# Expert layer in two sweeps: coefficients kept in two tensors by token half, 14 up tiles run for half the tokens first, and every second late down tile turned by VectorE

## Chip, cores and metric

One core of one Trainium2 chip runs the whole program. The metric is device microseconds (us) from the first to the last instruction of one execution, as a median of several. TensorE (PE) multiplies and can also transpose; VectorE (DVE), ScalarE (ACT) and GpSimd (POOL) do elementwise work; SyncE (SP) issues most loads; 16 DMA engines move the data.

## What is computed

Two transformer blocks on 256 tokens of width 1024. The change touches only the last part, a layer of 16,384 experts, of which each token uses 8 heads x 16:

```python
def peer_ffn(h, w_query, sub_keys1, sub_keys2, expert_down, expert_up):
    ...
    gates = jax.nn.softmax(top_v, axis=-1).astype(h.dtype)
    ...
        u = jnp.take(expert_down, idx_blk, axis=0)
        act = jax.nn.gelu(jnp.einsum('bpd,bphkd->bphk', h_blk, u))
        vv = jnp.take(expert_up, idx_blk, axis=0)
        return jnp.einsum('bphk,bphkd->bpd', g_blk * act, vv)
```

## The kernel before

The kernel does not gather experts. It computes all of them as 128 tiles of 128 experts and multiplies the unused ones by a coefficient of zero.

**Down sweep.** For each tile `n` the rows of `expert_down` (512 KB) are loaded, turned so that the model dimension lies on partitions, split into a high part (ACT, `dT_high`) and a low part (DVE, `dT_low`), and multiplied with the split tokens: 8 blocks x 3 products = 24 matmuls of 128x256 (`pe_three`, L577, L579, L581). ACT applies gelu and stores `G[:, n, :]`, 128 experts x 256 tokens (L2550). An ordinary tile is turned by PE, 8 transposes into two PSUM banks (L1189), done two tiles ahead: PE's order is turn(n+2), down(n). Tiles in `SQUARED` (n above 49 with n % 5 equal to 1 or 3, 31 tiles) are loaded in four pieces of 128 KB arranged so that DVE's 32x32 transposes finish the turn (L2011, L2012); PE has no turn for them. `dT_raw` of a squared tile lies where `dT_low` of the same third lay, so its turn waits for the matmuls of tile n-3. DVE's order is set by `v_tile`: the low part of tile n, then the turn of tile n+2 if that is squared.

**Coefficients.** While the sweep runs, POOL adds the gates into a DRAM matrix `C_dram` (expert x token, 16 MB, zeroed before) with 256 indirect DMAs: 8 heads x 2 token halves x 16 picks. A half of a head waits until the 16 adds of the head before it, for the same tokens, have landed.

**Up sweep.** For each tile `p` SP loads 128 rows of `expert_up` (512 KB) and the tile's coefficients (128 KB), each into one of 4 buffers. The up load of tile p waits for `tile_done` of tile p-4 (PE has finished it); the coefficient load of tile p+1 follows right behind it on SP. DVE multiplies `G` by the coefficients (`v_gate`, L2057), ACT copies the high parts (`up_high` L2558, `A_high` L2564), DVE subtracts for the low parts (L1318), and PE does 12 matmuls of 128x512 into four PSUM banks that add up over all tiles: banks 0 and 1 for tokens 0 to 127, banks 2 and 3 for the others. DVE's order is gate(p+1), low part of up tile p, low part of A for p. All engines run lists written out by hand, in order, with semaphores between them; no scheduler moves anything.

Of the kernel before, what the change touches and what calls it, by code (L numbers as in the profile page):

```python
# [15 lines left out]
P = 128  # L16
# [102 lines left out]
def program(nc, ctx, I, out):  # L119
# [368 lines left out]
    C_dram = nc.dram_tensor("c_dram", [N_KEYS * N_KEYS * S, 1], F32, kind="Internal").ap()  # L488
    turn_banks = ((4, 5), (0, 1), (2, 3))
    SQUARED = [n for n in range(N_KEYS) if n > 49 and n % 5 in (1, 3)]  # L490
# [713 lines left out]
    def pe_up_part(p, b):  # L1204
        t, at = b // 2, slice(b % 2 * CW, (b % 2 + 1) * CW)
        return pe_three(bank[b], A_low[p][:, t * P:(t + 1) * P], A_high[p % 4][:, t * P:(t + 1) * P],
                        up_low[p % 4][:, at], up_hi[p % 4][:, at], p == 0, p == N_KEYS - 1)

    def pe_tile_up(p):
        pe.wait_ge(weighed, p + 1)  # L1210
        pe.wait_ge(up_split, p + 1)
        for b in range(4):
            m = pe_up_part(p, b)
        m.then_inc(tile_done, 1)

    def pe_last_tiles():
        pe.wait_ge(weighed, N_KEYS)
        pe.wait_ge(up_split, N_KEYS)
        for b in range(4):
            pe_up_part(N_KEYS - 2, b)  # L1220
            pe_up_part(N_KEYS - 1, b).then_inc(bank_summed, 1)

    def pe_experts():
        pe_tile_turn(0)
        pe_tile_turn(1)
        for n in range(N_KEYS):
            if n + 2 < N_KEYS and n + 2 not in squared_at:
                pe_tile_turn(n + 2)
            pe_tile_down(n)
        for b in range(4):  # L1230
            fill(("acc", b), b)
        for p in range(N_KEYS - 2):
            pe_tile_up(p)
        pe_last_tiles()
# [726 lines left out]
    def v_picks(c, part, ts=range(TT), hs=range(PAIRS)):  # L1961
# [20 lines left out]
        else:  # L1982
            v_own.settle(v.scalar_tensor_tensor(rank[:, 0, rows], sel_key[:, 0, rows], float(N_KEYS), sel_key[:, 1, rows],
                                                ALU.mult, ALU.add))
            for t in ts:
                own = slice(PAIRS * t + hs.start, PAIRS * t + hs.stop)
                v.tensor_scalar(places[:, TP * c + own.start:TP * c + own.stop, :], rank[:, 0, own, :], float(S),
                                tokens[:, t:t + 1], ALU.mult, ALU.add).then_inc(picks_ready, 1)
# [30 lines left out]
    def v_tile(n):  # L2019
# [4 lines left out]
        if n + 2 in squared_at:  # L2024
            v_square_turn(n + 2)
# [28 lines left out]
    def v_gate(p):  # L2054
# [4 lines left out]
    def v_split_up(p):  # L2059
        v.wait_ge(up_high, p + 1)  # L2060
        v_low(up_low[p % 4], up_tile[p % 4], up_hi[p % 4]).then_inc(up_split, 1)

    def v_weigh(p):
        v.wait_ge(gated, p + 1)
        v.wait_ge(a_high_made, p + 1)
        v_low(A_low[p], G[:, p, :], A_high[p % 4]).then_inc(weighed, 1)

    def v_experts():
# [4 lines left out]
        for p in range(N_KEYS):  # L2073
            if p + 2 < N_KEYS:
                v_gate(p + 2)
            if p + 1 < N_KEYS:
                v_split_up(p + 1)
                v_weigh(p + 1)
# [473 lines left out]
    def a_split_up(p):  # L2552
        a.wait_ge(up_in[p % 4], 16 * (p // 4 + 1))
        if p > 3:
            a.wait_ge(tile_done, p - 3)
        else:
            held(a, ("down", N_KEYS - 3 + p // 2))
        a.copy(up_hi[p % 4].bitcast(F32R), up_tile[p % 4]).then_inc(up_high, 1)  # L2558

    def a_weigh(p):  # L2560
        a.wait_ge(gated, p + 1)
        if p > 3:
            a.wait_ge(tile_done, p - 3)
        a.copy(A_high[p % 4].bitcast(F32R), G[:, p, :]).then_inc(a_high_made, 1)  # L2564

    def a_experts():
# [16 lines left out]
        for p in range(1, N_KEYS):  # L2583
            a_weigh(p)
            a_split_up(p)
# [53 lines left out]

    def g_experts():  # L2640
        g.wait_ge(zeroed, 16)
        for c in range(4):
            for h in range(PAIRS * c, PAIRS * (c + 1)):
                for t in range(TT):
                    if c == 0:
                        g.wait_ge(picks_ready, 2 * (TT * h + t + 1))
                    elif h % PAIRS == 0:
                        g.wait_ge(picks_ready, 8 + 3 * c)
                    if h:
                        g.wait_ge(scattered[t][(h - 1) % 2], 16 * TOPK * ((h - 1) // 2 + 1))  # L2650
# [54 lines left out]
    def s_chunks():  # L2705
        for i, (name, w, c0, n) in enumerate(chunks):
# [125 lines left out]
```

## Time and profile before

| | |
|---|---|
| median of 3 runs | 1539.0 us (1538.61 to 1540.46) |
| profiled execution | 1540.89 us, span 1539.6 us |
| PE busy | 1500.0 us, 97% of the span |
| DVE, ACT, POOL busy | 1081.1, 657.8, 434.8 us |
| mean granted TensorE clock | 0.992 of full speed |

The span is the time between the first and the last instruction in the trace; the execution's own time is 1.3 us more. A busy share is an average over very different stages. The down sweep ends and the up sweep begins at about 1183 us of the span.

### The profile page before, as it was taken

What the parts mean: (1) busy time and instruction counts of PE and PEld (TensorE: products, weight loads), DVE (VectorE), ACT (ScalarE), POOL (GpSimd) and SP (SyncE); (2) the same over time, 40 slices, a digit from 0 to 9 for tenths busy, and PEclk for the clock granted to TensorE, in tenths of its full rate; (3) what the DMA queues carried; (4) which work ended last, traced back from release to release, by engine and by line L of the source; (5) the groups of instructions that cost most, each with busy time, mean ns of one, the idle gap of its engine ahead of it and who ended that gap; (6) DMA issues with size and microseconds to landing.
All of it is one profiled execution on the core that took longest, in us unless ns stands there. A gap on an engine that the chain in (4) does not pass through costs nothing.

```text
span 1539.6 us, 25208 instructions
## 1 busy us (share of the span) xinstructions
PE 1500.0 (97%) x9851; PEld 1264.4 (82%) x9851; DVE 1081.1 (70%) x1895; ACT 657.8 (43%) x982; POOL 434.8 (28%) x285
## 2 busy tenths in 40 slices
PE   8999999999999888999999999999999999999998
PEld 5777878875755577599999999999999888888887
DVE  5788788664765754667988875656556777777776
ACT  4456453643321511343444443334334445455453
POOL 0000000000010200028888888888884000000000
PEclk9999999999999989999999999999999999999999
DMA  9777574357555920356767666666664777777776
GB/s 343 270 244 247 193 259 138 137 191 250 193 197 177 397 88 22 137 165 186 144 138 147 142 139 158 144 164 144 159 152 109 239 240 240 238 240 240 239 241 232
DMA packets 179850, 297.24 MB, mean 193 GB/s; under 512 B 51434, under 2 KB 88066, under 8 KB 179732
## 3 DMA queue, kind: packets, MB, share of 16 engines
q1 hardware_dynamic: 133072, 277.08, 53.8%
q0 software_dynamic: 39296, 8.55, 8.0%
q10 hardware_dynamic: 7364, 9.99, 2.0%
q8 instruction: 79, 1.29, 0.3%
q14 instruction: 39, 0.32, 0.1%
HBM read 276.54 MB, written 19.03 MB: 192 GB/s over the span
## 4 chain that ended last, share of the span: by engine, by line
PE 87%; DVE 5%; ACT 3%; issue 2%; DMA 2%; ACTq 1%; DVEq 0%
PE bank L577 22%; PE bank L579 22%; PE bank L581 21%; PE bank L1189 6%; PE bank L572 5%; PE bank L1120 1%; ACTq L2101 1%; PE bank L1136 1%; PE bank L549 1%; PE bank L927 1%; DVE gt L1299 1%; PE bank L939 1%; PE bank L938 1%; DVE w_low L1318 1%; PE bank L629 1%
## 5 line engine op out<-in xcount | busy, mean ns | idle before, releaser
L2653 POOL DMA_INDIRECT c_dram<-gates,places x256 | 412.4, 1611 | 149.6 <-issue 77.7
L577 PE MATMUL bank<-hT_high,dT_high 128*128 128x256 f32 x1024 | 296.0, 289 | 0.0
L579 PE MATMUL bank<-hT_low,dT_high 128*128 128x256 f32 x1024 | 289.0, 282 | 0.0
L581 PE MATMUL bank<-hT_high,dT_low 128*128 128x256 f32 x1024 | 285.6, 279 | 0.0
L2558 ACT CAST up_high<-slot 128x1024 fp32r<-128x1024 f32 x128 | 134.3, 1049 | 157.8 <-DMA slot<-in_expert_up_dram 157.8
L577 PE MATMUL bank<-up_high,A_high 128*128 128x512 f32 x512 | 200.0, 391 | 1.0 <-DVE A_low L1318 1.0
L579 PE MATMUL bank<-up_low,A_high 128*128 128x512 f32 x512 | 200.7, 392 | 0.0
L581 PE MATMUL bank<-up_high,A_low 128*128 128x512 f32 x512 | 199.2, 389 | 0.0
L577 PEld LDWEIGHTS bank<-hT_high,dT_high 128*128 128x128 f32 x1024 | 192.8, 188 | 4.6 <-issue 0.2
L581 PEld LDWEIGHTS bank<-hT_high,dT_low 128*128 128x128 f32 x1024 | 193.5, 189 | 0.0
L579 PEld LDWEIGHTS bank<-hT_low,dT_high 128*128 128x128 f32 x1024 | 192.6, 188 | 0.0
L1318 DVE TENSOR_TENSOR up_low<-slot,up_high 128x1024 fp32r<-128x1024 f32 x128 | 156.8, 1225 | 32.9 <-ACT up_high L2558 32.5
L2190 ACT CAST w_hi<-slot 128x2048 fp32r<-128x2048 f32 x51 | 97.0, 1902 | 137.7 <-PE bank L581 95.4
L1318 DVE TENSOR_TENSOR w_low<-slot,w_hi 128x2048 fp32r<-128x2048 f32 x51 | 116.7, 2288 | 45.6 <-ACT w_hi L2190 45.4
L1318 DVE TENSOR_TENSOR dT_low<-bank,dT_high 128x512 fp32r<-128x512 f32 x194 | 123.3, 677 | 25.7 <-ACT dT_high L2546 24.5
L577 PE MATMUL bank<-w_hi,h_hi 128*128 128x512 f32 x344 | 138.2, 402 | 0.0
L579 PE MATMUL bank<-w_low,h_hi 128*128 128x512 f32 x344 | 136.4, 396 | 0.0
L581 PE MATMUL bank<-w_hi,h_lo 128*128 128x512 f32 x344 | 135.3, 393 | 0.0
L2550 ACT ACTIVATE G<-bank 128x256 f32<-128x256 f32 x128 | 49.1, 384 | 194.0 <-PE bank L581 194.0
L577 PEld LDWEIGHTS bank<-up_high,A_high 128*128 128x128 f32 x512 | 96.2, 188 | 23.1 <-DVE A_low L1318 1.4
L581 PEld LDWEIGHTS bank<-up_high,A_low 128*128 128x128 f32 x512 | 96.1, 188 | 21.2
L579 PEld LDWEIGHTS bank<-up_low,A_high 128*128 128x128 f32 x512 | 96.1, 188 | 20.5
(454 smaller groups left out, 2545.9 us busy)
## 6 DMA issues: line engine op xcount, KB each, us to landing
slot<-in_expert_up_dram SPq DMA_DIRECT2D x128, 512.0 KB, 3.5
slot<-in_expert_down_dram SPq DMA_DIRECT2D x97, 512.0 KB, 3.7
slot<-in_w_in_dram SPq DMA_DIRECT2D x41, 1024.0 KB, 5.2
P<-in_w_ada_dram SPq DMA_DIRECT2D x16, 1024.0 KB, 7.9
c_dram<-zeros SPq DMA_DIRECT2D x1, 16384.0 KB, 50.9
slot<-c_dram SPq DMA_DIRECT2D x128, 128.0 KB, 3.4
slot<-in_expert_down_dram SPq DMA_DIRECT2D x124, 128.0 KB, 2.8
slot<-in_w_in_dram SPq DMA_DIRECT2D x6, 2048.0 KB, 8.9
```

What stands on the lines that cost most here:

```text
L549: m = pe.transpose(b[:, n * P:(n + 1) * P], tiles[k * size + n], ident)
L572: m = pe.matmul(sums, lhsT=lhs[:, k, t * P:(t + 1) * P], rhs=w[:, k, :], start=(k == 0), stop=(k == w.shape[1] - 1))
L577: pe.matmul(o, lhsT=lhs_high.bitcast(F32R), rhs=rhs_high.bitcast(F32R), start=start, stop=False, skip_group_check=True)
L579: pe.matmul(o, lhsT=lhs_high.bitcast(F32R), rhs=rhs.bitcast(F32R), start=False, stop=False, skip_group_check=True)
L581: return pe.matmul(o, lhsT=lhs.bitcast(F32R), rhs=rhs_high.bitcast(F32R), start=False, stop=stop, skip_group_check=True)
L629: pe.matmul(row, lhsT=col[:, 0:1], rhs=ada_acc[r % 2], start=True, stop=True).then_inc(filled(("ada", r)), 1)
L1189: m = pe.transpose(b[:, k * P:(k + 1) * P], spread_block(down_tile[n % 3], 4 * k4 + k), ident)
L1318: return v.tensor_tensor(dst.bitcast(F32R), src, high, ALU.subtract)
L2190: a.copy(w_hi[w_high_at[h]].bitcast(F32R), half_view(h)).then_inc(w_high, 1)
L2550: a.activation(G[:, n, :], b, ACT.Gelu_apprx_tanh).then_inc(emptied(("down", n)), 1)
L2558: a.copy(up_hi[p % 4].bitcast(F32R), up_tile[p % 4]).then_inc(up_high, 1)
L2653: g.indirect_dma_start(C_dram, bass.IndirectOffsetOnAxis(ap=places[:, x, k:k + 1], axis=0), gates[:, x, k:k + 1], None, compute_op=ALU.add ...
```

## The change

Four edits go together. `C_dram` becomes two tensors, one for each half of the tokens, zeroed by two DMAs; a coefficient load of a full tile becomes two of 64 KB. The last heads are scattered in another order: head 7 of the first half now comes before the second half of head 6's adds for the other tokens. The up sweep becomes a list of 142 `passes`: first up tiles 0 to 13 for tokens 0 to 127 alone; then the full tiles 14 to 127, and ahead of tile 14 and of every fourth tile after it one of tiles 0 to 13 for tokens 128 to 255. Every pass loads its whole up tile, so 14 tiles are loaded and split twice. And `SQUARED` becomes every odd tile above 49 (39 tiles), with DVE turning tile n+1, not n+2, behind the low part of tile n.

```diff
-    C_dram = nc.dram_tensor("c_dram", [N_KEYS * N_KEYS * S, 1], F32, kind="Internal").ap()
+    C_dram = [nc.dram_tensor(f"c_dram{t}", [N_KEYS * N_KEYS * P, 1], F32, kind="Internal").ap() for t in range(TT)]
+    AHEAD, BOTH = 14, range(TT)
+    passes = [(p, range(1)) for p in range(AHEAD)]
+    for p in range(AHEAD, N_KEYS):
+        if (p - AHEAD) % 4 == 0 and (p - AHEAD) // 4 < AHEAD:
+            passes.append(((p - AHEAD) // 4, range(1, TT)))
+        passes.append((p, BOTH))
+    first_pass = [min(u for u, (p, ts) in enumerate(passes) if t in ts) for t in range(TT)]
...
-    SQUARED = [n for n in range(N_KEYS) if n > 49 and n % 5 in (1, 3)]
+    SQUARED = [n for n in range(N_KEYS) if n > 49 and n % 2 == 1]
...
+    def pe_tile_up(u):
+        pe.wait_ge(weighed, u + 1)
+        pe.wait_ge(up_split, u + 1)
+        for t in passes[u][1]:
+            for b in (2 * t, 2 * t + 1):
+                m = pe_up_part(u, b)
+        m.then_inc(tile_done, 1)
...
-        if n + 2 in squared_at:
-            v_square_turn(n + 2)
+        if n + 1 in squared_at:
+            v_square_turn(n + 1)
...
+    def v_gate(u):
+        p, tok = passes[u][0], up_tokens(u)
         clear(v, ("down", p))
-        v.wait_ge(coeff_in[p % 4], 16 * (p // 4 + 1))
-        v.tensor_tensor(G[:, p, :], G[:, p, :], coeff[p % 4], ALU.mult).then_inc(gated, 1)
+        v.wait_ge(coeff_in[u % 4], 16 * sum(len(passes[x][1]) for x in range(u % 4, u + 1, 4)))
+        v.tensor_tensor(G[:, p, tok], G[:, p, tok], coeff[u % 4][:, tok], ALU.mult).then_inc(gated, 1)
...
+        for h in range(PEER_H - 2):
+            for t in range(TT):
+                g_head(h, t)
+        g_head(PEER_H - 2, 0)
+        g_head(PEER_H - 2, 1, range(TOPK // 2))
+        g_head(PEER_H - 1, 0)
+        g_head(PEER_H - 2, 1, range(TOPK // 2, TOPK))
+        g_head(PEER_H - 1, 1)
...
+    def s_up(u):
+        p = passes[u][0]
+        if u > 3:
+            sp.wait_ge(tile_done, u - 3)
+        sp.dma_start(up_tile[u % 4], I["expert_up_2"][0][p * P:(p + 1) * P, :]).then_inc(up_in[u % 4], 16)
+
+    def s_coeff(u):
+        p, ts = passes[u]
+        for t in ts:
+            if u == first_pass[t]:
+                for h in range(2):
+                    sp.wait_ge(scattered[t][h], 16 * TOPK * PEER_H // 2)
+        if u > 3:
+            sp.wait_ge(gated, u - 3)
+        for t in ts:
+            sp.dma_start(coeff[u % 4][:, t * P:(t + 1) * P],
+                         C_dram[t][p * P * P:(p + 1) * P * P].rearrange("(e n) o -> e (n o)", n=P)).then_inc(coeff_in[u % 4], 16)
...
-        for t in range(TT):
-            sp.wait_ge(scattered[t][1], 16 * TOPK * PEER_H // 2)
-        for p in range(4):
-            s_coeff(p)
-        for p in range(4, N_KEYS):
-            s_coeff(p)
-            s_up(p)
+        for u in range(4):
+            s_coeff(u)
+        for u in range(4, len(passes)):
+            s_coeff(u)
+            s_up(u)
```

Here is DVE's list from tile 49 of the down sweep on, before. `dT_low_201`, `_203` and `_199` are the three buffers of low parts; a row with `bank` belongs to a tile that PE turned, a row with `dT_raw` to a squared tile.

```order
L1318 TENSOR_TENSOR dT_low_201<-bank,dT_high_202 128x512 x2
L2011 STREAM_TRANSPOSE dT_raw_352<-slot_51 128x512
L2012 STREAM_TRANSPOSE dT_raw_352<-slot_51 128x512
L1318 TENSOR_TENSOR dT_low_203<-bank,dT_high_204 128x512 x2
L1318 TENSOR_TENSOR dT_low_199<-dT_raw_352,dT_high_200 128x1024
L2011 STREAM_TRANSPOSE dT_raw_356<-slot_51 128x512
L2012 STREAM_TRANSPOSE dT_raw_356<-slot_51 128x512
L1318 TENSOR_TENSOR dT_low_201<-bank,dT_high_202 128x512 x2
L1318 TENSOR_TENSOR dT_low_203<-dT_raw_356,dT_high_204 128x1024
```

The same place with the change:

```order
L1331 TENSOR_TENSOR dT_low_201<-bank,dT_high_202 128x512 x2
L1331 TENSOR_TENSOR dT_low_203<-bank,dT_high_204 128x512 x2
L2024 STREAM_TRANSPOSE dT_raw_352<-slot_51 128x512
L2025 STREAM_TRANSPOSE dT_raw_352<-slot_51 128x512
L1331 TENSOR_TENSOR dT_low_199<-dT_raw_352,dT_high_200 128x1024
L1331 TENSOR_TENSOR dT_low_201<-bank,dT_high_202 128x512 x2
L2024 STREAM_TRANSPOSE dT_raw_356<-slot_51 128x512
L2025 STREAM_TRANSPOSE dT_raw_356<-slot_51 128x512
L1331 TENSOR_TENSOR dT_low_203<-dT_raw_356,dT_high_204 128x1024
```

The two transposes of a squared tile stood between the low parts of the two tiles before it; now they stand behind both, directly ahead of the squared tile's own low part.

PE's list at the start of the up sweep, before, where `up_high_341` and `A_high_206` belong to up tile 0:

```order
L577 MATMUL bank<-up_high_341,A_high_206 128x512
L579 MATMUL bank<-up_low_194,A_high_206 128x512
L581 MATMUL bank<-up_high_341,A_low_213 128x512
L577 MATMUL bank<-up_high_341,A_high_206 128x512
L579 MATMUL bank<-up_low_194,A_high_206 128x512
L581 MATMUL bank<-up_high_341,A_low_213 128x512
L577 MATMUL bank<-up_high_341,A_high_206 128x512
```

And with the change:

```order
L589 MATMUL bank<-up_high_341,A_high_206 128x512
L591 MATMUL bank<-up_low_194,A_high_206 128x512
L593 MATMUL bank<-up_high_341,A_low_213 128x512
L589 MATMUL bank<-up_high_341,A_high_206 128x512
L591 MATMUL bank<-up_low_194,A_high_206 128x512
L593 MATMUL bank<-up_high_341,A_low_213 128x512
L589 MATMUL bank<-up_high_342,A_high_207 128x512
```

Tile 1 (`up_high_342`) begins after 6 matmuls of tile 0, not 12; the other 6 come later, with a second load of the tile.

## Rows read from the trace of the kernel before

**Rows 1.** Stretches: us, busy PE, PEld, DVE, ACT, POOL, PEclk, DMA share, GB/s.

```profile
1190.00:1516.00 326.00, 326.00 (x1426) 267.46 (x1425) 233.87 (x356) 162.49 (x238) 0.00 (x0) 1.00 0.74 240
380.00:390.00 10.00, 7.73 (x31) 4.98 (x30) 8.62 (x27) 5.32 (x20) 0.00 (x0) 1.00 0.42 155
536.00:538.00 2.00, 0.22 (x6) 0.22 (x8) 1.97 (x5) 0.32 (x1) 0.00 (x0) 1.00 1.04 399
538.00:540.00 2.00, 1.44 (x32) 1.25 (x28) 1.93 (x5) 0.52 (x1) 0.00 (x0) 0.55 1.05 408
```

**Rows 2.** Timeline of ACT, gelus of tiles 43 and 48 (start us, us, operation).

```profile
892.15 0.39 ACT L2550 ACTIVATE G<-bank 128x256 f32<-128x256 f32 x1 [2.16 <-PE bank L581]
...
910.84 0.38 ACT L2550 ACTIVATE G<-bank 128x256 f32<-128x256 f32 x1 [2.15 <-PE bank L581]
```

**Rows 3.** Timeline of ACT, gelus of tiles 126 and 127.

```profile
1179.93 0.38 ACT L2550 ACTIVATE G<-bank 128x256 f32<-128x256 f32 x1 [2.44 <-PE bank L581]
...
1182.76 0.38 ACT L2550 ACTIVATE G<-bank 128x256 f32<-128x256 f32 x1 [1.20 <-PE bank L581]
```

**Rows 4.** Timeline of ACT around squared tile 96: gelu 93, high part 96, gelu 98.

```profile
1066.52 0.38 ACT L2550 ACTIVATE G<-bank 128x256 f32<-128x256 f32 x1 [2.15 <-PE bank L581]
1068.98 1.05 ACT L2541 CAST dT_high<-dT_raw 128x1024 fp32r<-128x1024 f32 x1 [2.07 <-DVE dT_raw L2012]
...
1083.82 0.38 ACT L2550 ACTIVATE G<-bank 128x256 f32<-128x256 f32 x1 [2.15 <-PE bank L581]
```

**Rows 5.** Timeline of DVE there: turn of 96 (its first half), low parts of 95 and 96.

```profile
1066.60 1.21 DVE L2011 STREAM_TRANSPOSE dT_raw<-slot 128x512 f32<-128x512 f32 x1 [4.65 <-PE bank L581]
...
1068.82 1.24 DVE L1318 TENSOR_TENSOR dT_low<-bank,dT_high 128x512 fp32r<-128x512 f32 x2
1070.06 1.23 DVE L1318 TENSOR_TENSOR dT_low<-dT_raw,dT_high 128x1024 fp32r<-128x1024 f32 x1
```

**Rows 6.** Timeline of PE there: turn of tile 97, first matmul of tile 95.

```profile
1069.15 1.06 PE L1189 MATMUL bank<-ident,slot 128*128 128x128 f32 x8
1070.20 0.36 PE L577 MATMUL bank<-hT_high,dT_high 128*128 128x256 f32 x1
```

**Rows 7.** Timeline of PE where the up sweep begins: tile 127's last, up tiles 0 and 1.

```profile
1182.44 0.28 PE L581 MATMUL bank<-hT_high,dT_low 128*128 128x256 f32 x1
1183.10 0.47 PE L577 MATMUL bank<-up_high,A_high 128*128 128x512 f32 x1 [0.38 <-DVE A_low L1318]
...
1186.03 0.50 PE L577 MATMUL bank<-up_high,A_high 128*128 128x512 f32 x1
```

**Rows 8.** Timeline of POOL: the last scatter.

```profile
1171.87 1.55 POOL L2653 DMA_INDIRECT c_dram<-gates,places  x1 [0.30 <-issue]
```

**Rows 9.** Timelines of SP, ACT, DVE: up tile 10, load of 11, gate of 12.

```profile
1202.81 0.33 SPq L2765 DMA_DIRECT2D slot<-in_expert_up_dram  x1
...
1205.56 0.33 SPq L2765 DMA_DIRECT2D slot<-in_expert_up_dram  x1
...
1206.23 1.05 ACT L2558 CAST up_high<-slot 128x1024 fp32r<-128x1024 f32 x1 [1.33 <-DMA slot<-in_expert_up_dram]
...
1207.31 1.23 DVE L1318 TENSOR_TENSOR up_low<-slot,up_high 128x1024 fp32r<-128x1024 f32 x1 [0.28 <-ACT up_high L2558]
1208.46 0.42 DVE L1318 TENSOR_TENSOR A_low<-G,A_high 128x256 fp32r<-128x256 f32 x1
1210.83 0.42 DVE L2057 TENSOR_TENSOR G<-G,slot 128x256 f32<-128x256 f32 x1 [1.96 <-DMA slot<-c_dram]
```

**Rows 10.** DMA queues, packets, MB, share: 1207.5 to 1210.5 us, then 1190 to 1516 us.

```profile
q8 instruction: 1, 0.02, 2.0%
...
q8 instruction: 11, 0.18, 0.2%
```

**Rows 11.** Groups by line and shape: count, busy us, mean ns, idle before.

```profile
L1940 DVE TENSOR_TENSOR cand<-best 128x512 f32<-128x512 f32 x6 | 4.1, 680 | 0.0
L1318 DVE TENSOR_TENSOR A_low<-G,A_high 128x256 fp32r<-128x256 f32 x128 | 53.5, 418 | 0.0
```

More of the change, by code:

```diff
@@ L1231, in pe_experts @@
             fill(("acc", b), b)
-        for p in range(N_KEYS - 2):
-            pe_tile_up(p)
+        for u in range(len(passes) - 2):
+            pe_tile_up(u)
         pe_last_tiles()
@@ L1986, in v_picks @@
                 own = slice(PAIRS * t + hs.start, PAIRS * t + hs.stop)
-                v.tensor_scalar(places[:, TP * c + own.start:TP * c + own.stop, :], rank[:, 0, own, :], float(S),
-                                tokens[:, t:t + 1], ALU.mult, ALU.add).then_inc(picks_ready, 1)
+                v.tensor_scalar(places[:, TP * c + own.start:TP * c + own.stop, :], rank[:, 0, own, :], float(P),
+                                tokens[:, 0:1], ALU.mult, ALU.add).then_inc(picks_ready, 1)
             v.wait_ge(gate_exp, group_at(c, ts, hs) + 1)
@@ L2072, in v_experts @@
         v_weigh(0)
[L2073 to L2078, printed above, removed]
+        for u in range(len(passes)):
+            if u + 2 < len(passes):
+                v_gate(u + 2)
+            if u + 1 < len(passes):
+                v_split_up(u + 1)
+                v_weigh(u + 1)
         v.wait_ge(x_in, 32)
@@ L2550, in a_tile_gelu, with a_split_up, a_weigh @@
         a.activation(G[:, n, :], b, ACT.Gelu_apprx_tanh).then_inc(emptied(("down", n)), 1)
[L2552 to L2555, printed above, removed]
-        else:
[L2557 to L2564, printed above, removed]
+    def a_split_up(u):
+        a.wait_ge(up_in[u % 4], 16 * (u // 4 + 1))
+        if u > 3:
+            a.wait_ge(tile_done, u - 3)
+        else:
+            held(a, ("down", N_KEYS - 3 + u // 2))
+        a.copy(up_hi[u % 4].bitcast(F32R), up_tile[u % 4]).then_inc(up_high, 1)
+    def a_weigh(u):
+        p, tok = passes[u][0], up_tokens(u)
+        a.wait_ge(gated, u + 1)
+        if u > 3:
+            a.wait_ge(tile_done, u - 3)
+        a.copy(A_high[u % 4][:, tok].bitcast(F32R), G[:, p, tok]).then_inc(a_high_made, 1)
     def a_experts():
@@ L2582, in a_experts @@
                 a_gates(n // 15)
-        for p in range(1, N_KEYS):
-            a_weigh(p)
-            a_split_up(p)
+        for u in range(1, len(passes)):
+            a_weigh(u)
+            a_split_up(u)
     a_first_block()
@@ L2720, in s_chunks @@
                 sp.wait_ge(zeros_set, 1)
-                sp.dma_start(C_dram.rearrange("(p a b) o -> p a (b o)", p=P, b=CW),
-                             zeros.unsqueeze(1).broadcast_to([P, N_KEYS * S // CW, CW])).then_inc(zeroed, 16)
+                for t in range(TT):
+                    sp.dma_start(C_dram[t].rearrange("(p a b) o -> p a (b o)", p=P, b=CW),
+                                 zeros.unsqueeze(1).broadcast_to([P, N_KEYS * P // CW, CW])).then_inc(zeroed, 16)
     def s_tail():
```

81 lines of the change are left out of this document (36 added, 45 removed).

## The prediction

> **What bounds the kernel now.** I read the stretches first. From 1190 to 1516 us, nearly the whole up sweep, PE is busy all of 326 us at full granted clock, while the 16 DMA engines are at 0.74 and move 240 GB/s [rows 1]. So here PE sets the end, and what counts is when it begins and whether it is kept fed. For the down sweep I read the gelus of ACT, since ACT waits for PE there and one gelu follows each tile. Where PE turns every tile, five tiles take 910.84 - 892.15 = 18.69 us, 3.74 each [rows 2]; where it turns none, a tile takes 2.83 us [rows 3]. One turn by PE costs 0.91 us.
>
> With squared tiles in the mix the sum does not close. From gelu 93 to gelu 98 five tiles take 17.30 us [rows 4], in which PE makes three turns: 5 x 2.83 + 3 x 0.91 = 16.88. The missing 0.42 us, for two squared tiles, is a wait that no list of waits shows. PE began the turn of tile 97 at 1069.15, and at 0.91 us for eight transposes it was through at 1070.06; its next matmul, of tile 95, starts at 1070.20 and is 0.36 long [rows 6] where such a matmul takes 0.28 [rows 7]. DVE had only then, at 1068.82 + 1.24 = 1070.06, finished the low part of 95, because the two transposes of squared tile 96 stood ahead of it, and they could not start before 1066.60 [rows 5]. Thus each squared tile costs PE some 0.2 us, late by the order on DVE.
>
> **Squares and their order.** From gelu 48 (910.84 [rows 2]) to gelu 127 (1182.76 [rows 3]) 79 tiles take 271.9 us. With the change PE turns 38 tiles in this stretch, where it turned 46: 38 x 3.74 + 41 x 2.83 = 258.1 us. That is 13.8 us less: 8 x 0.91 = 7.3 from turns, and 6.5 (31 x 0.21) if the wait goes too. Does it? The turn of squared tile s may start when tile s-3 is through. Then come its transposes (1068.82 - 1066.60 = 2.2 us, with 0.15 to start), ACT's high part (1.05 [rows 4]) and DVE's low part (1.23): ready after about 4.8 us. PE meanwhile does tile s-2, a turn and tile s-1: 2.83 + 0.91 + 2.83 = 6.6 us. Room of 1.7 us; and DVE, with the 1.24 of the next ordinary tile behind it, is done after 6.1, before the next squared turn may start at 6.6. I take the whole 13.8; the bounds are 7.3, if the pairs lose as much as squared tiles do now, and 13.8. DVE's eight more tiles (2.2 of transposes each) and SP's three more issues for each lie in this cover; without it a pair would last 6.6 plus what is over.
>
> **Scatters.** The down sweep would end 13.8 us sooner, at 1182.56 - 13.8 = 1168.8 (the last matmul starts at 1182.44 [rows 7], plus its slot of 0.12). The last scatter is issued at 1171.87 and lasts 1.55 [rows 8], so a sweep over whole tiles could not begin; the first half of the tokens has its last adds 24 scatters earlier, some 45 us at 1.86 each. The other half may end a few us later than now, since its last 16 wait for the 8 just before. It is first read for pass 14, by a load that SP reaches after pass 9, 20 us into the up sweep, about 1189. So the scatters cost nothing; they would have to be over 10 us late to matter. The second zeroing DMA lies far ahead.
>
> **The first 14 passes.** PE needs 2.75 us for a full pass (the loads come at that step, 1205.56 - 1202.81 [rows 9]) and 1.37 for a half. But a pass has to be fed: from the issue of up load 10 to the end of its A low part go 1208.88 - 1202.81 = 6.07 us (load 3.4, ACT 1.05, DVE the rest) [rows 9], and the load into a buffer is issued when PE has finished the pass four before. With three full passes between that leaves 8.2 us, and PE never waits; with three half passes it leaves 4.1. Four passes then take 6.07 less 0.14 for the smaller A, plus 1.37, plus about 0.3 for the restart and the semaphores: 7.6 us, 1.91 each. (A half of 128x256, 0.42 us, is bounded by 0.21 and 0.42; the step from 128x512 to 128x256 is 0.68 to 0.42 [rows 11], so I take 0.28.) The start goes by DVE: up tile 1 starts 1186.03 - 1182.56 = 3.5 us into the sweep now [rows 7], 3.3 with the smaller pieces; passes 2 to 4 follow at DVE's own step, 1.15 + 2 x 0.28 = 1.7 us; pass 4 starts at 8.4 and pass 14 at 8.4 + 10 x 1.91 = 27.5, with about 1 us more until full passes run back to back. Now, PE does the same matmuls in 14 x 1.37 = 19.2 us and loses 0.9 (0.54 ahead of tile 0, the rest ahead of tile 1 [rows 7]). **Loss: 28.5 - 20.1 = 8.4 us.**
>
> The loads then come at 0.59 MB in 1.91 us, 309 GB/s, against 240 now; 408 GB/s was reached elsewhere [rows 1]. If a load lands 0.3 us later for it, the ten passes cost 10 x 0.3 / 4 = 0.8 us. I take that; the bounds are 0 and, with 0.6 later, 1.5.
>
> **The mixed part.** After that one half pass goes with four full ones, 14 times. DVE and ACT have room: 4 x 2.0 + 1.7 us of DVE work in 12.4. But of five passes three have the half pass among the three ahead of them, and their feeding time falls from 8.0 to 2 x 2.75 + 1.37 - 0.2 = 6.7 us. The chain takes 6.1 and, by a second coefficient issue of 0.3 to 0.4 ahead of the gate, up to 0.2 more; room of 0.4. Sometimes it is later: the gate of tile 12 waited 1.96 us for coefficients whose load had been issued right behind 1205.56, so that the low part of A for tile 11 ended about 7.2 us after its load's issue [rows 9], and in those 3 us an instruction fetch of 16 KB ran on queue q8 [rows 10]. Of such fetches there are 11 in 326 us, one in ten passes. Today's room swallows them. In the 173 us of the mixed part there are some 6; three in five meet a short one and cost 0.5 + 0.1 to restart, more with the slower landings. **I take 2.5 us**, between 0 and 6. Behind it, full passes have their old room and both coefficient issues fit.
>
> **Sum.** -13.8 + 8.4 + 0.8 + 2.5 = -2.1 us on the profiled 1540.9 us, so 1538.8; the median lies 1.9 under the profiled execution. I forecast a median of 1537.0 us.
>
> **Rivals.**
> 1. *The feeding goes better:* loads land as fast as now and fetches find room. Then -13.8 + 8.0 + 0 to 1 gives -5.5: 1533.5 us. For it: the engines' share of 0.74 leaves space. Against it: the room of 0.4 us is smaller than the lateness seen.
> 2. *Landing is slower under load (the other side):* at 309 GB/s, and then at 260 in the mixed part, a load takes 4.0 us, not 3.4. The half sweep costs 8.4 + 1.5, and in the mixed part three of five passes are fed after 6.7 + 0.2, so that each group loses some 0.4 to 0.5: 14 x 0.45 = 6.3, and 3 for the fetches. -13.8 + 9.9 + 9.3 = +5.4: 1544.4 us. It decides from a landing of about 3.8 us on. For it: the share is 1.03 and more wherever 400 GB/s are moved, so the engines queue somewhere between. Against it: a load comes every 1.9 us and its own pieces need less.
> 3. *The wait in the pairs stays,* since DVE has only 0.5 us to spare: the gain is 7.3, the rest as forecast: +4.4, 1543.4 us. It decides once DVE's five operations and the wait for ACT take over 6.6 us a pair. Against it: the sum of 6.1 from rows.
> 4. *The clock falls in the half sweep.* After PE had been busy 0.22 of 2 us the granted clock fell to 0.55 in the next two, from 2.4 towards 1.2 GHz, but in another stretch with PE busy 7.73 of 10 us it stayed at 1.00 [rows 1]. The half sweep would have PE busy about 70% of each pass, with waits of 0.2 to 1.2 us. At half clock a half pass takes 2.75 us, PE sets the step, and 14 passes last 38.5 us, not 28: +10, 1547 us. The Trainium skill (TensorE: Matmul & The Clock Gate, "HAM oscillation — how this bites in real kernels") describes such a loop, in which a short group of matmuls alternates with a wait for the next load and the clock is lost every time; by that the whole half sweep would be slow. The stretch with 7.73 of 10 us busy speaks against it here, so I give it little.
> 5. *The change doesn't free the start:* if the second half's scatters ended after 1199, pass 14 would wait for them. They would have to be 25 us late.
>
> **How the numbers follow.** The forecast with its own range of 1534.5 to 1540.5 gets 0.54, rival 1 0.20, rival 2 0.12, rival 3 0.08, rival 4 0.04, rival 5 0.02. A measurement of this kernel tells a difference of 0.2% (3.1 us) from none. All of rival 1 and a third of the forecast's share, with its better half of the bounds, lie below 1535.9: faster 0.37. Rivals 2 to 5, less the part of 2 and 3 that stops short, lie above 1542.1: slower 0.22. The rest, 0.41, is the same. The range from 1532 to 1544 leaves out the worse half of rival 2, the clock and the scatters.
>
> **What would show it.** In the down sweep two tiles should take 6.57 us between gelus of the same kind, and DVE's turn should stand right before the squared low part, with PE never late; 6.8 or more speaks for rival 3. Tile 127 should end near 1169 us. In the up sweep the first half pass should start 0.5 us later, and the half passes, from the fifth on, should follow in groups of four that last 7.6 us, with PE waiting for the low parts of up tile or A; a load should land in 3.4 to 3.8 us. Pass 14 should begin 27 to 29 us after tile 127. In the mixed part PE's waits should sum to 1 to 4 us and stand in the three passes behind a half pass. I am wrong if the half passes run at 1.4 us (a loss of 8 us that isn't there, 1529 us), if the granted clock leaves 1.00, or if DVE falls behind in the pairs.

## The result, and the profile after

The changed kernel takes 1563.6 us (1560.7 to 1566.6, four executions) against 1539.1 for the kernel before: a ratio of 1.0158, with a 95% interval from 1.0137 to 1.0178. It is 24 us slower, where 2 us faster was forecast. The profiled execution took 1563.35 us, its span is 1562.0.

The first view is ACT's timeline at the gelus of tiles 48 and 127, which answers to [rows 2, 3]:

```profile
908.38 0.38 ACT L2565 ACTIVATE G<-bank 128x256 f32<-128x256 f32 x1 [2.15 <-PE bank L593]
...
1166.39 0.38 ACT L2565 ACTIVATE G<-bank 128x256 f32<-128x256 f32 x1 [1.31 <-PE bank L593]
```

The stretch lasts 258.0 us, 13.9 less than before. That part came as forecast, so the loss lies behind it. The page's chain of work, which was PE for 87% before, now goes through POOL's scatters, and of the groups the scatters (256 in both kernels, 412.4 us busy before) have grown by 33.5 us:

```profile
PE 51%; POOL 28%; issue 7%; DVE 5%; DMA 5%; ACT 2%; ACTq 1%; SPq 0%; DVEq 0%; POOLq 0%
...
L2666 POOL DMA_INDIRECT c_dram<-gates,places x256 | 445.9, 1742 | 152.0 <-issue 77.4
```

Next the timeline where the half sweep meets pass 14, the first for the other half of the tokens: the last scatter on POOL (it answers to [rows 8]), SP's two issues on either side of its wait (the up tile of pass 13, then the coefficients of pass 14), DVE's gate of pass 14, and PE's first matmul of pass 13.

```profile
1187.76 0.33 SPq L2791 DMA_DIRECT2D slot<-in_expert_up_dram  x1
...
1205.56 1.55 POOL L2666 DMA_INDIRECT c_dram<-gates,places  x1 [0.30 <-issue]
...
1208.60 0.32 SPq L2802 DMA_DIRECT2D slot<-c_dram  x1
...
1210.48 0.29 DVE L2071 TENSOR_TENSOR G<-G,slot 128x128 f32<-128x128 f32 x1 [17.92 <-DMA slot<-c_dram]
...
1212.17 0.79 PE L589 MATMUL bank<-up_high,A_high 128*128 128x512 f32 x1 [17.89 <-DVE A_low L1331]
```

SP stands ready at 1188, but the last scatter ends at 1207.11, 33.7 us later than before. The load follows 1.5 us after it and PE 5.1 us after it, having waited 17.9 us. The pass that waits on PE is 13, not 14: 13 half passes have run, and the up tile of pass 13 is there and copied by ACT (its `up_high` starts at 1192.09). But DVE's list has gate(p+1) ahead of the low parts for p, so the gate of pass 14, which needs the late coefficients, also keeps back pass 13. The stretches show what the wait did to the clock (us of the window, busy time and count for PE, PEld, DVE, ACT, POOL, then granted clock, DMA share, GB/s):

```profile
1168.00:1190.00 22.00, 15.99 (x60) 10.48 (x60) 16.90 (x31) 12.67 (x21) 16.86 (x8) 1.00 0.92 254
1190.00:1207.00 17.00, 3.60 (x14) 2.10 (x12) 2.57 (x5) 2.40 (x3) 14.33 (x9) 0.78 0.25 15
1207.00:1214.00 7.00, 1.83 (x4) 1.49 (x5) 2.08 (x5) 1.40 (x3) 0.11 (x1) 0.50 0.61 164
1214.00:1220.00 6.00, 5.16 (x17) 3.35 (x16) 5.29 (x8) 3.07 (x5) 0.00 (x0) 0.79 0.98 305
```

In the half passes themselves (1168 to 1190) it stayed at 1.00. It fell only with the wait, to 0.50, the lower of the two levels. The first matmul behind the wait took 0.79 us, those after it 0.63, and from 1216.72 on they took 0.39 again.

Why are the scatters late? Here POOL's and DVE's timelines in two neighbouring pairs of tiles:

```profile
1131.56 1.55 POOL L2666 DMA_INDIRECT c_dram<-gates,places  x1 [0.30 <-issue]
1133.42 1.55 POOL L2666 DMA_INDIRECT c_dram<-gates,places  x1 [0.30 <-issue]
1135.27 2.57 POOL L2666 DMA_INDIRECT c_dram<-gates,places  x1 [0.30 <-issue]
1138.14 1.56 POOL L2666 DMA_INDIRECT c_dram<-gates,places  x1 [0.30 <-issue]
1140.01 1.55 POOL L2666 DMA_INDIRECT c_dram<-gates,places  x1 [0.30 <-issue]
1141.87 2.51 POOL L2666 DMA_INDIRECT c_dram<-gates,places  x1 [0.30 <-issue]
...
1135.17 1.22 DVE L1331 TENSOR_TENSOR dT_low<-dT_raw,dT_high 128x1024 fp32r<-128x1024 f32 x1 [1.17 <-ACT dT_high L2556]
1136.31 1.28 DVE L1331 TENSOR_TENSOR dT_low<-bank,dT_high 128x512 fp32r<-128x512 f32 x2
1138.28 1.21 DVE L2024 STREAM_TRANSPOSE dT_raw<-slot 128x512 f32<-128x512 f32 x1 [0.69 <-PE bank L593]
...
1141.73 1.22 DVE L1331 TENSOR_TENSOR dT_low<-dT_raw,dT_high 128x1024 fp32r<-128x1024 f32 x1 [1.17 <-ACT dT_high L2556]
```

A scatter that begins while DVE computes the low part of a squared tile lasts up to 2.57 us instead of 1.55, and it ends 1.42 to 1.45 us after that operation's end, in every such case of this trace: here 1135.27 + 2.57 = 1137.84, and the operation ends at 1135.17 + 1.22 = 1136.39. The operation has two operands in SBUF (`dT_raw`, `dT_high`); the low part of an ordinary tile reads one from PSUM (`bank`), and of the 74 scatters that begin beside it or beside the transposes after 720 us none takes more than 1.56. Nor is it chance which scatter is met. A held one costs 1.0 us more, three steps of 1.86 us follow, 6.57 in all, and that is exactly one pair of tiles. So the third scatter behind a held one again begins 0.1 us after the next low part. After 720 us there are 44 above 2 us, 2.50 on average: 37 held by the low part of a squared tile, 6 by the low part of an up tile in the half sweep (`slot` and `up_high`, also two operands in SBUF), 1 by another operation of DVE. The kernel before has the same hold, shorter and rarer (15 above 2 us):

```profile
1060.06 2.12 POOL L2653 DMA_INDIRECT c_dram<-gates,places  x1 [0.30 <-issue]
...
1069.91 1.56 POOL L2653 DMA_INDIRECT c_dram<-gates,places  x1 [0.30 <-issue]
...
1059.53 1.22 DVE L1318 TENSOR_TENSOR dT_low<-dT_raw,dT_high 128x1024 fp32r<-128x1024 f32 x1
1060.67 0.68 DVE L1318 TENSOR_TENSOR dT_low<-bank,dT_high 128x512 fp32r<-128x512 f32 x1
```

There nine steps of 1.86 and a hold of 0.57 make the 17.3 us of five tiles. A scatter that begins before the operation isn't held: beside the low part that starts at 1070.06 [rows 5] stands one that begins at 1069.91 and takes 1.56. That is how the kernel before met only every other low part: they follow each other after 10.53 and 6.77 us in turn, and five steps behind a held scatter the next one begins some 0.1 us ahead of the operation.

The up sweep after pass 14 loses time too. PE's timeline at the first half pass, the first pass of the mixed part, the first pass behind it, and the last matmul:

```profile
1166.60 0.47 PE L589 MATMUL bank<-up_high,A_high 128*128 128x512 f32 x1 [0.24 <-DVE A_low L1331]
...
1215.46 0.79 PE L589 MATMUL bank<-up_high,A_high 128*128 128x512 f32 x1 [0.37 <-DVE A_low L1331]
...
1398.08 0.39 PE L589 MATMUL bank<-up_high,A_high 128*128 128x512 f32 x1
...
1558.12 0.39 PE L593 MATMUL bank<-up_high,A_low 128*128 128x512 f32 x1
```

Of PE's steady step a half takes 1.373 us (6 x 0.2288). The half sweep needs 14 x 1.373 = 19.2 us and lasted 48.9: 29.6 over. The mixed part, 14 x 9 halves, needs 173.0 and lasted 182.6: 9.6 over. "Over" means this below.

### The profile page after: what moved, and what is told of

Read it like the earlier page. It is cut to its first block, busy times and chain, and to the rows that moved or that the text cites. A ratio compares the mean times of both kernels' runs of the same rounds, so it can differ in the third digit from the quotient of the medians.

```text
span 1562.0 us, 25372 instructions
## 1 busy us (share of the span) xinstructions
PE 1493.7 (96%) x9787; PEld 1251.8 (80%) x9787; DVE 1118.3 (72%) x1945; ACT 673.6 (43%) x1002; POOL 468.4 (30%) x285
## 4 chain that ended last, share of the span: by engine, by line
PE 51%; POOL 28%; issue 7%; DVE 5%; DMA 5%; ACT 2%; ACTq 1%; SPq 0%; DVEq 0%; POOLq 0%
POOL c_dram L2666 28%; PE bank L589 13%; PE bank L591 12%; PE bank L593 12%; PE bank L584 4%; DMA slot<-c_dram 2%; DMA ada_late<-in_w_ada_dram 1%; DMA slot<-in_expert_up_dram 1%; ACTq L2116 1%; PE bank L939 1%; PE bank L561 1%; PE bank L951 1%; DVE gt L1312 1%; PE bank L641 1%; PE bank L950 1%
## 5 line engine op out<-in xcount | busy, mean ns | idle before, releaser
L2666 POOL DMA_INDIRECT c_dram<-gates,places x256 | 445.9, 1742 | 152.0 <-issue 77.4
L589 PE MATMUL bank<-up_high,A_high 128*128 128x512 f32 x512 | 204.6, 400 | 30.1 <-DVE A_low L1331 29.7
L2573 ACT CAST up_high<-slot 128x1024 fp32r<-128x1024 f32 x142 | 149.0, 1049 | 161.0 <-DMA slot<-in_expert_up_dram 161.0
L1331 DVE TENSOR_TENSOR up_low<-slot,up_high 128x1024 fp32r<-128x1024 f32 x142 | 173.9, 1225 | 28.3 <-ACT up_high L2573 27.3
L1331 DVE TENSOR_TENSOR dT_low<-bank,dT_high 128x512 fp32r<-128x512 f32 x178 | 114.4, 684 | 28.3 <-ACT dT_high L2561 27.2
L2071 DVE TENSOR_TENSOR G<-G,slot 128x256 f32<-128x256 f32 (+1 forms) x142 | 56.5, 398 | 92.1 <-DMA slot<-c_dram 91.0
```

Of the source, the lines that this page charges most:

```text
L589: pe.matmul(o, lhsT=lhs_high.bitcast(F32R), rhs=rhs_high.bitcast(F32R), start=start, stop=False, skip_group_check=True)
L1331: return v.tensor_tensor(dst.bitcast(F32R), src, high, ALU.subtract)
L2071: v.tensor_tensor(G[:, p, tok], G[:, p, tok], coeff[u % 4][:, tok], ALU.mult).then_inc(gated, 1)
L2573: a.copy(up_hi[u % 4].bitcast(F32R), up_tile[u % 4]).then_inc(up_high, 1)
L2666: g.indirect_dma_start(C_dram[t], bass.IndirectOffsetOnAxis(ap=places[:, x, k:k + 1], axis=0), gates[:, x, k:k + 1], None, compute_op=ALU. ...
```

## Experiments

Theory 1: the loss is the scatters that DVE's low part holds, and behind that the feeding of half passes. Rivals stand with each run. The times of all runs beside the kernel before on the same chip:

| run | median us | ratio (95%) | last scatter ends | first up matmul | half sweep, mixed part over |
|---|---|---|---|---|---|
| changed kernel | 1563.6 | 1.0158 (1.0137 to 1.0178) | 1207.1 | 1166.6 | 29.6, 9.6 |
| e1_squares_only | 1565.8 | 1.0173 (1.0156 to 1.0190) | 1198.1 | 1204.3 | none |
| e2_passes_only | 1560.8 | 1.0143 (1.0126 to 1.0160) | 1173.1 | 1179.0 | 10.7, 10.1 |
| e3_old_tiles_new_order | 1556.1 | 1.0106 (1.0089 to 1.0123) | 1196.2 | 1171.1 | 13.9, 13.4 |
| e4_turn_to_psum | 1549.0 | 1.0058 (1.0041 to 1.0075) | 1163.0 | 1165.7 | 10.9, 9.6 |
| e10_low_in_four | 1546.7 | 1.0063 (1.0048 to 1.0078) | 1170.0 | 1172.0 | 10.3, 15.4 |
| e7_psum_one_load | 1545.0 | 1.0039 (1.0024 to 1.0054) | 1163.9 | 1166.6 | 11.3, 8.6 |
| e9_no_second_load | 1540.6 | 0.9997 (0.9984 to 1.0010) | 1166.8 | 1169.9 | 10.2, 4.9 |
| e6_psum_four_ahead | 1534.4 | 0.9968 (0.9956 to 0.9979) | 1165.8 | 1168.5 | 2.3, 4.2 (four) |
| e8_psum_two_loads | 1532.1 | 0.9961 (0.9946 to 0.9975) | 1164.3 | 1171.6 | none |
| e5_psum_whole_passes | 1528.1 | 0.9928 (0.9915 to 0.9941) | 1163.7 | 1170.0 | none |

**e1_squares_only**, the kernel before with the new squares and their order:

```diff
-    SQUARED = [n for n in range(N_KEYS) if n > 49 and n % 5 in (1, 3)]
+    SQUARED = [n for n in range(N_KEYS) if n > 49 and n % 2 == 1]
...
-        if n + 2 in squared_at:
-            v_square_turn(n + 2)
+        if n + 1 in squared_at:
+            v_square_turn(n + 1)
```

> The kernel before with the squares of the change alone: every odd tile above 49, turned one tile ahead; one coefficient tensor, old scatter order, whole passes. Theory 1 (a scatter that would start while DVE computes the low part of a squared tile, which reads two operands from SBUF, is held until that operation ends): the down sweep ends 13 to 14 us sooner, near 1168, one scatter in three takes 2.5 us as with the change, the last one ends near 1205, PE starts the up sweep some 29 us later than before, near 1212: 1568 us. Rival, the two half tensors or the new order of the last heads slow the scatters: here they take 1.61 us on average as before, end near 1173, and the up sweep starts a few us sooner: 1536 us.

Measured 1565.8 us. 38 scatters are above 2 us, 37 of them held by the low part of a squared tile; the last ends 24.6 us later than before, and as a sweep over whole passes needs them all, PE waits 37.4 us for its first tile; in the 10 us behind that wait the granted clock is 0.69. Two edits that make the down sweep 14 us shorter make the kernel 27 us slower, without any half pass.

**e2_passes_only**, the changed kernel with the old squares and the old order:

```diff
-    SQUARED = [n for n in range(N_KEYS) if n > 49 and n % 2 == 1]
+    SQUARED = [n for n in range(N_KEYS) if n > 49 and n % 5 in (1, 3)]
...
-        if n + 1 in squared_at:
-            v_square_turn(n + 1)
+        if n + 2 in squared_at:
+            v_square_turn(n + 2)
```

> The change with the old squares and the old place of their turn: only the two tensors, the order of the last heads and the 142 passes. Theory 1: scatters 1.61 us on average as before, the last one ends near 1177, no wait at pass 14; the half sweep costs 8 to 9 us and the mixed part 4 to 5: 1552 us. Rival (two tensors or order): scatters 1.74 us on average here too, pass 14 waits for them, 1560 us or more.

Measured 1560.8 us. The scatters are those of the kernel before (17 above 2 us, the last ends at 1173.14), so two tensors and the new order of heads don't slow them, and no pass waits for them. But the time is 9 us above the 1552 that theory 1 gave: the mixed part costs 10.1 us, not 4 to 5, and the half sweep 10.7, not 8 to 9.

**e3_old_tiles_new_order**, the changed kernel with the old squares alone (first two lines of the diff above).

> The change with the 31 squared tiles of before, but each turned one tile ahead as in the change. Five tiles should take 16.9 us, not 17.3, so the down sweep ends some 6.5 us sooner than before. Theory 1: nine scatters need 16.7 us, so one per cycle is held for about 0.2 us only, and all end near 1172 to 1177; pass 14 does not wait: 1539 - 6.5 + 13 = 1545 us. Rival, any tile turned ahead by one slows the scatters whatever the number: one scatter of 2.5 us for each squared tile, 31 in all, the last one ends 20 us later than before and pass 14 waits.

Measured 1556.1 us: with the same 31 squared tiles as before, 34 scatters are above 2 us, 28 of them held by the low part of a squared tile, and pass 13 waits 3.1 us. The form of theory 1 that had one short hold in each five tiles is wrong, and the rival is right: nearly each squared tile holds a scatter, and the last one ends 23 us later. What brings a scatter into each low part is where the order puts that operation in the scatters' step. The low parts now follow each other after 10.3 and 6.57 us in turn, and both fit a hold of 1.0 with whole steps of 1.86, five and three. Here a scatter begins 0.07 us after the low part at 1061.01:

```profile
1061.08 2.58 POOL L2666 DMA_INDIRECT c_dram<-gates,places  x1 [0.30 <-issue]
...
1061.01 1.23 DVE L1331 TENSOR_TENSOR dT_low<-dT_raw,dT_high 128x1024 fp32r<-128x1024 f32 x1 [1.17 <-ACT dT_high L2556]
```

The order also gives its gain here. Gelus 48 to 127 take 265.3 us, 6.6 less than before with as many turns by PE: the 6.5 of the hidden waits.

**e4_turn_to_psum**, the changed kernel with the transposes written to PSUM, so that the low part has one operand in SBUF:

```diff
-        v.transpose(dT_raw[n % 3][:, 0:half * P], x[:, 0:half])
-        v.transpose(dT_raw[n % 3][:, half * P:], x[:, half:]).then_inc(down_turned, 1)
+        v.transpose(bank[turn_banks[n % 3][0]], x[:, 0:half])
+        v.transpose(bank[turn_banks[n % 3][1]], x[:, half:]).then_inc(down_turned, 1)
...
-        v_low(dT_low[n % 3].rearrange("p k n -> p (k n)"), dT_raw[n % 3],
-              dT_high[n % 3].rearrange("p k n -> p (k n)")).then_inc(turned_low, 1)
+        for k4 in range(2):
+            ...
+            m = v_low(dT_low[n % 3][:, at, :], bank[turn_banks[n % 3][k4]].rearrange("p (k n) -> p k n", k=4),
+                      dT_high[n % 3][:, at, :])
+        m.then_inc(turned_low, 1)
...
```

> The change, but DVE writes the turned squared tile to the two PSUM banks that PE's turn would use, so the high and low parts read it from PSUM in two pieces and the low part has only one operand in SBUF. Same transposes, same order. Theory 1: no scatter is held, all take 1.55 us (1.86 from start to start), the last one ends near 1166; pass 14 does not wait; down sweep as with the change: 1539 - 14 + 13 = 1538 us. Rival, DVE's transposes or its mere business hold POOL: one scatter in three stays at 2.5 us, the time stays near 1563 us.

Measured 1549.0 us, 14.6 less than the changed kernel. One scatter is above 2 us after 720, beside another operation of DVE with two operands in SBUF; the group lost 42 us, and the last ends at 1162.98, before the down sweep:

```profile
L2671 POOL DMA_INDIRECT c_dram<-gates,places x256 | 403.7, 1577 | 152.4 <-issue 77.4 <-DVE gates L2005 71.4 <-DMA c_dram<-gates,places 3.6
```

No pass waits for the scatters any more; the half sweep is 10.9 us over instead of 29.6. The time is 11 us above theory 1's figure. 7 of them are the mixed part. In the trace PE also waits 3.65 us ahead of the last two passes, for the last up tile, which ACT could take only 6.4 us after its load was issued. e6's trace has such a wait too (2.73), e2's and e10's a smaller one (1.75 and 1.19); in the others, the kernel before and the changed one among them, it is under 0.8. Why was not found.

**e10_low_in_four**, the changed kernel with the low part cut and both operands left in SBUF:

```diff
-        v_low(dT_low[n % 3].rearrange("p k n -> p (k n)"), dT_raw[n % 3],
-              dT_high[n % 3].rearrange("p k n -> p (k n)")).then_inc(turned_low, 1)
+        low, high = (x[n % 3].rearrange("p k n -> p (k n)") for x in (dT_low, dT_high))
+        for piece in range(4):
+            at = slice(256 * piece, 256 * piece + 256)
+            m = v_low(low[:, at], dT_raw[n % 3][:, at], high[:, at])
+        m.then_inc(turned_low, 1)
```

> The changed kernel with only the low part of a squared tile cut: four operations of 128x256 in place of one of 128x1024, both operands in SBUF as before. Theory 1a (a scatter is held by the one operation that is running when it comes, and gets in between two): a hold is at most the 0.42 us of such an operation, scatters over 2 us vanish, the last one ends between 1163 and 1180 us instead of 1207, pass 14 waits for nothing, and the time is e4's, 1549 us (to 1552, if four operations make the pairs longer). Theory 1b (it is held as long as such operations follow each other): 44 scatters of about 2.5 us stay, the last ends near 1207, 1563 us.

Measured 1546.7 us. A scatter gets in between two of the four. The longest beside them is 1.80 us. Here the longest of a 20 us stretch, which began 0.84 us into the four and took 0.15 more than 1.55:

```profile
1108.63 1.70 POOL L2669 DMA_INDIRECT c_dram<-gates,places  x1 [0.30 <-issue]
...
1107.79 1.43 DVE L1331 TENSOR_TENSOR dT_low<-dT_raw,dT_high 128x256 fp32r<-128x256 f32 x4 [1.17 <-ACT dT_high L2559]
```

The mean scatter is 1.587 us, gelus 48 to 127 still take 258.0. So the hold lasts as long as the one operation that was running, and four short ones cost DVE 0.2 us more and POOL almost nothing. (The profiled execution, 1555.65 us, is the slowest of the six: its mixed part was 15.4 us over.)

The Trainium skill (SBUF — State Buffer, "Who interferes with whom") says that a DVE instruction with two SBUF inputs contends with a GpSimd instruction that reads SBUF, and, of DVE's two-port modes, that whoever issues first gets the shared ports "for the whole instruction". The traces agree where DVE comes first: the scatter is held to the end of the operation (1.0 us with the long one, 0.15 with a short one). Where the scatter came first they show no hold of DVE: the low part at 1070.06 began 0.15 us into a scatter and took its usual 1.23 us. The same section reports that `tensor_tensor` did not stall a DMA issued by GpSimd; here such an operation held the indirect ones, up to 44 times, and the measurement decides.

**e5_psum_whole_passes**, the kernel before with the edits of e1 and e4 alone: one coefficient tensor, whole passes.

> The kernel before, with only the odd late tiles squared (turned one tile ahead, transposes into PSUM as in e4_turn_to_psum): one coefficient tensor, whole passes, no half of a pass ahead. Theory 1 (no scatter is held any more, so the last one ends near 1163 us as in e4; the half passes cost what e4's trace shows, 20.4 us over the matmuls): the first whole pass starts 5.1 us after the last scatter, as pass 14 did in the changed kernel (1207.1 to 1212.2), near 1168 instead of 1182.4, and the time is 1525 us (1522 to 1530). Rival (the half passes cost only the 11.7 us that the prediction gave them): e4's 1549 less 11.7 and plus the 2.4 us of later start, 1540 us.

Measured 1528.1 us, 11 us faster than the kernel before, and 35 faster than the changed one. Last scatter, last gelu of the down sweep and first up matmul:

```profile
1162.10 1.55 POOL L2658 DMA_INDIRECT c_dram<-gates,places  x1 [0.30 <-issue]
...
1169.40 0.38 ACT L2555 ACTIVATE G<-bank 128x256 f32<-128x256 f32 x1 [1.20 <-PE bank L581]
...
1169.96 0.47 PE L577 MATMUL bank<-up_high,A_high 128*128 128x512 f32 x1 [0.59 <-DVE A_low L1318]
```

The scatters end 6 us before the down sweep, and PE goes over with a wait of 0.59 us. The rival, half passes at the price that the prediction gave them, falls.

**e8_psum_two_loads** and **e6_psum_four_ahead** are e4 with another number of passes ahead:

```diff
-    AHEAD, BOTH = 14, range(TT)
+    AHEAD, BOTH = 0, range(TT)
```

and 4 in the other.

> e4_turn_to_psum with no half passes: two coefficient tensors, each whole pass loads both, scatters in the changed order. Against e5_psum_whole_passes it shows what two tensors alone cost. Theory 1 (later landings cost nothing where whole passes leave 0.5 us of slack each, as the rest of e4's up sweep shows): same as e5, 1525 us, up to 1531 if the late last tile of e4 comes with the two loads. Rival (the two loads are the dear part): 1535 us or more.

> e4_turn_to_psum with 4 passes' first half ahead instead of 14. Theory 1 (each pass that is cut in two costs 1.45 us, 0.77 where its first half runs and 0.68 where its second half runs, as e4's trace shows: 10.9 and 9.45 us for 14): ten fewer give 14.5 us back, 1534.5 us (1529 where the 5.7 us that e4 lost before its last two passes is gone too). Rival (the 9.45 us of the mixed part come with the two coefficient loads of each whole pass, not with the half passes): only 7.7 us come back, 1541 us.

Measured 1532.1 and 1534.4 us. Without half passes, two tensors cost 4 us against e5, at the start: SP issues ten coefficient loads in a row, 4.62 us, where e5 issues five in 2.91; PE's first wait is 4.66 us, and its first pass takes 2.2 us too long.

```profile
1165.94 4.62 SPq L2807 DMA_DIRECT2D slot<-c_dram  x10
...
1171.56 0.77 PE L589 MATMUL bank<-up_high,A_high 128*128 128x512 f32 x1 [4.66 <-DVE A_low L1331]
```

Later the up tiles land after 4.6 us instead of 3.5, and whole passes lose nothing by it. From 0 to 4 to 14 passes ahead the time goes 1532.1, 1534.4, 1549.0: 1.1 to 1.2 us for each (by the ratios and by the times), less at first, where four of them cover e8's wait.

**e7_psum_one_load** is e4 with the coefficients laid out as before, in one tensor:

```diff
-        for t in ts:
-            sp.dma_start(coeff[u % 4][:, t * P:(t + 1) * P],
-                         C_dram[t][p * P * P:(p + 1) * P * P].rearrange("(e n) o -> e (n o)", n=P)).then_inc(coeff_in[u % 4], 16)
+        rows = C_dram[p * P * S:(p + 1) * P * S].rearrange("(e n) o -> e (n o)", n=S)
+        sp.dma_start(coeff[u % 4][:, up_tokens(u)], rows[:, up_tokens(u)]).then_inc(coeff_in[u % 4], 16)
...
```

> e4_turn_to_psum with one coefficient tensor, laid out as in the kernel before: a whole pass loads its coefficients in one transfer of 1 KB rows instead of two of 512 B rows; half passes load half of each row. Theory A (the up tiles land later, 4.6 us instead of 3.5, because of the two loads, and that is what the mixed part's 9.45 us instead of 2.5 come from): landing back near 3.5 us, mixed part near 3 us, time 1542 us, 1536 where the 5.7 us before the last two passes go too. Theory B (a half pass costs what ACT and DVE need for it over its matmuls, whatever the loads): mixed part still 9 us, time 1548 us, 1543 with the last passes back.

Measured 1545.0 us. The last passes are back to normal, but the mixed part is 8.6 us over as before: the two loads are not its cause. With them gone, up tiles still land after 4.2 us:

```profile
slot<-in_expert_up_dram SPq DMA_DIRECT2D x75, 512.0 KB, 4.2
```

**e9_no_second_load** is e7 without the second load of the 14 tiles; ACT and DVE split a piece of `G` in its place:

```diff
         if u > 3:
             sp.wait_ge(tile_done, u - 3)
+        if passes[u][1] == range(1, TT):
+            return
...
+    def up_source(u):
+        if passes[u][1] == range(1, TT):
+            return G[:, 120:124, :].rearrange("p k n -> p (k n)")
+        return up_tile[u % 4]
...
```

> e7_psum_one_load, but the 14 passes for the second half of the tokens load no up tile: ACT and DVE split 128x1024 elements of G (tiles 120 to 123) in its place, with the same instructions, so that the output is wrong in these 14 tiles' second half. Theory C (the mixed part's 8.4 us are up tiles that land too late, since a half pass leaves the loads behind it 1.4 us less time and adds a fifth load to every four): without that load the step of the loads is 3.1 us instead of 2.5, landing falls from 4.2 to about 3.5, and the mixed part loses 2 to 3 us: 1539 us. Theory B (a half pass costs what ACT, DVE and the semaphores need for it): the mixed part keeps its 8 us, 1545 us.

Measured 1540.6 us, with the ratio's interval wholly below e7's. PE, ACT and DVE have the same instructions, yet the mixed part is 4.9 us over instead of 8.6, 1.8 of it in its first pass.

```profile
slot<-in_expert_up_dram SPq DMA_DIRECT2D x63, 512.0 KB, 3.7
```

So the second loads cost 3.7 us of the mixed part in these two traces, somewhat more than the 2 to 3 of theory C. The 4.9 that stay look like the fetches of the prediction: 4.2 of them stand within 8 us behind one of the seven 16 KB instruction fetches (queue q8) around that stretch. One example: queue q8 in the window from 1278 to 1280 us (packets, MB, share), DVE's gate that then waits for coefficients, and PE:

```profile
q8 instruction: 1, 0.02, 2.7%
...
1281.24 0.42 DVE L2074 TENSOR_TENSOR G<-G,slot 128x256 f32<-128x256 f32 x1 [2.22 <-DMA slot<-c_dram]
...
1283.19 0.50 PE L589 MATMUL bank<-up_high,A_high 128*128 128x512 f32 x1 [0.52 <-DVE A_low L1331]
```

In e7's trace 2.4 of the 8.6 us stand so, and 6.2 elsewhere, where e9 has 0.8. This is a coincidence in time: no run took the fetches away, so their share is not shown.

## Why the prediction was wrong

The step that failed first is **Scatters**, "So the scatters cost nothing; they would have to be over 10 us late to matter." The condition was near enough, but the lateness was put at "a few us" without asking what sets POOL's pace: the end of the last scatter was taken over from the kernel before [rows 8], as if DVE's new order could not move it. One number spoke against that: a single scatter takes 1.55 us [rows 8], but the group's mean is 1611 ns, 15.6 us more over 256 scatters. After 720 us the scatters take 9.6 us more than their usual 1.555, and 8.5 of them are holds by the low part of a squared tile, the very operation that the change makes more frequent and moves. With the change the 9.6 became 43.3 us, 37.0 by squared tiles and 4.8 by the half passes' own low parts, and 3.1 us of waiting for head 7 came on top (the "few us" of the forecast). The last scatter ended 34 us later, PE waits 17.9 us ahead of pass 13, and the half sweep costs 18.8 more than in e4, clock included. Rival 5 names the wait, with 0.02, but not its cause, which no rival has. The prediction also gave two limits, 10 us late here and 25 in rival 5. The trace puts it near 16: PE was through with pass 12 at 1194.3, 5.1 us go from the last scatter to PE, and the old end is 1173.4.

**Squares and their order**: right. 258.0 us for 258.1, pairs of 6.57 us, and e3 shows the hidden wait's share apart, 6.6 for 6.5. Rival 3 falls.

**The first 14 passes**: right in size, with a wrong landing. Undisturbed (e4) they cost 10.4 us more than the same matmuls in the kernel before, against 8.4 + 0.8, each reckoned from the end of the down sweep. But four passes last 9.0 to 9.2 us there, not 7.6: the ten loads land after 4.4 us (4.6 in the changed kernel), not 3.4 to 3.8. That makes 3.2 us more for ten passes, of which the 0.8 and the 1 us that the sum had set aside took up most. The granted clock stayed at 1.00 while the half passes ran; rival 4 falls.

**The mixed part** is the second step that failed, a term mis-sized: 9.6 us for 2.5 (8.6 to 10.1 in three other traces, 13.4 and 15.4 in two). The losses stand where the prediction put them, 8.3 of 9.6 ahead of the three passes behind a half pass. But the room of 0.4 us was reckoned with the landing of 3.4 us of whole passes; it was 4.4 here. So the feeding was late without a fetch too: 5.8 of the 9.6 us stand further than 8 us behind any (1.2 of them in the first pass, where the clock was still low), and e9 shows 3.7 us as the second loads' share. Rival 2 said this, with its limit at 3.8 us, and its 9.9 and 9.3 us are close to what the two parts cost. In part that is luck, since it reckoned with 4.0 and with 3 us of fetches that no run shows apart. Without the scatters' lateness the change ends at 1549.0 us in e4 and 1546.7 in e10, 0.6% slower than before, and the three other terms alone make +6.1 us: that too lies above the range of 1532 to 1544.

Added up on the profiled executions: -2.5 before the gelu of tile 48, where the runs scatter from 905.6 to 913.8 us, then -13.9 + 10.4 + 18.8 + 9.6, in all +22.4, against 22.5 measured (the medians are 24.5 apart). Of the miss, 18.8 us are the scatters, 7.1 the mixed part and 1.2 the half sweep.

## What to carry to other kernels

A shorter stage is worth only what the slowest of its companions lets through, and that companion's own pace may hang on the work that was moved: look at the mean of its group against its minimum, and explain the difference before taking its end as fixed. Here one operand in PSUM, or an operation cut in four, freed some 40 us of POOL's time at almost no cost. An engine with an ordered list can also hold back work that is ready: one gate for pass 14 stopped pass 13. A pass cut in two is fed twice, which cost 15 to 17 us for 14 of them here, so it pays only where the engine would wait longer than that anyway; whole passes on the freed scatters were the fastest kernel.

## What was not expected of the hardware

- DVE held POOL's indirect DMAs: 1.55 us alone, up to 2.57 when begun during a 1.22 us operation with two SBUF operands. In the kernel before 15 scatters began 0.10 to 0.14 us ahead of such an operation: all took 1.55 or 1.56 us, and the operations their 1.23.
- A hold can lock itself in: 1.0 + 3 x 1.86 us is the 6.57 us of a pair, so nearly every pair held one scatter; with cuts or PSUM 256 ran at 1.58 to 1.59 on average.
- After a wait of 17.9 us the granted clock was 0.50 (1207 to 1214 us) and PE's matmuls took 0.63 us for 0.39, until 4.5 us behind the wait; the half passes, with waits of up to 1.23 us between them, kept 1.00.
